# Which engine makes the low parts of the expert weights: VectorE alone, or VectorE with one in twelve on GpSimd

## The reference, cut to what matters

```
def moe_ffn(h, router, w1, w3, w2):              # h: 256 tokens x 1024
    logits = (t @ router).astype(float32)
    top_v, top_i = lax.top_k(logits, TOP_K)      # 2 of 8
    top_w = softmax(top_v)
    gates = sum(one_hot(top_i, 8) * top_w[..., None], axis=1)
    for e in range(N_EXPERTS):
        out = out + gates[:, e:e + 1] * (silu(t @ w1[e]) * (t @ w3[e])) @ w2[e]
```

## Time and profile before

| what | value |
|---|---|
| median of 3 runs | 1508.79 us (1505.52 to 1510.47) |
| the profiled execution: its time, its span | 1508.79 us, 1507.1 us |
| PE busy over the span | 1450.7 us (96%) |
| DVE | 1264.5 us (84%) |
| ACT | 1099.1 us (73%) |
| POOL | 91.9 us (6%) |
| DMA, mean over the span | 310 GB/s |
| DMA, in the expert stage from 700 to 1400 us | 416 GB/s |

### The profile page before, as it was taken

How to read it: one execution, slowest core, us unless ns; L and a number is a source line. 1 busy time by engine, 2 the same in 40 slices (tenths; PEclk the granted TensorE clock), 3 DMA queues, 4 the chain that set the end, 5 groups by cost and what they waited for, 6 DMA issues and landing times.

```text
span 1507.1 us, 22229 instructions
## 1 busy us (share of the span) xinstructions
PE 1450.7 (96%) x8401; PEld 1258.1 (83%) x8401; DVE 1264.5 (84%) x1414; ACT 1099.1 (73%) x1315; POOL 91.9 (6%) x48
## 2 busy tenths in 40 slices
PE   7999989999999999899999999999999999999996
PEld 7999969999899998788877877787877887778774
DVE  5887775455578868789999999999999999999996
ACT  5685553333547663588888888888898889898885
POOL 4000000000000000000000031000040000040001
PEclk9999999999999999999999999999999999999999
DMA  9545345555344443989999999999999999999993
GB/s 276 204 148 188 141 154 210 193 177 189 140 169 176 176 156 138 389 325 422 411 421 408 409 420 416 421 420 408 411 413 423 421 409 407 422 415 421 421 420 106
DMA packets 66439, 467.02 MB, mean 310 GB/s; under 512 B 7658, under 2 KB 7894, under 8 KB 11030
## 3 DMA queue, kind: packets, MB, share of 16 engines
q1 hardware_dynamic: 63878, 458.27, 76.0%
q0 software_dynamic: 2400, 7.24, 2.4%
q10 hardware_dynamic: 48, 0.02, 0.0%
HBM read 460.26 MB, written 5.24 MB: 309 GB/s over the span
## 4 chain that ended last, share of the span: by engine, by line
PE 71%; DVE 19%; ACT 6%; issue 2%; DMA 1%; POOL 0%; ACTq 0%; DVEq 0%
DVE w_lo L653 12%; PE bank L843 9%; PE bank L1150 9%; PE bank L844 9%; PE bank L845 9%; PE bank L1151 9%; PE bank L1154 9%; PE bank L1106 4%; PE bank L1103 4%; PE bank L1115 1%; ACT w_hi L581 1%; PE bank L1219 1%; ACT w_hi L647 1%; DVE w_lo L589 1%; PE bank L896 1%
## 5 line engine op out<-in xcount | busy, mean ns | idle before, releaser
L653 DVE TENSOR_TENSOR w_lo<-arena,w_hi 128x1024 fp32r<-128x1024 f32 x528 | 617.7, 1218 | 28.9 <-ACT w_hi L647 23.9
L647 ACT ACTIVATE w_hi<-arena 128x1024 fp32r<-128x1024 f32 x528 | 533.6, 1054 | 59.4 <-PE bank L1154 56.1
L589 DVE TENSOR_TENSOR w_lo<-ring,w_hi 128x2048 fp32r<-128x2048 f32 x94 | 214.9, 2290 | 129.7 <-ACT w_hi L581 128.7
L843 PE MATMUL bank<-h_hi,w_hi 128*128 128x256 f32 x992 | 283.2, 285 | 1.9 <-DVE h_lo L1729 1.7
L844 PE MATMUL bank<-h_lo,w_hi 128*128 128x256 f32 x992 | 280.6, 283 | 0.0
L845 PE MATMUL bank<-h_hi,w_lo 128*128 128x256 f32 x992 | 280.6, 283 | 0.0
L581 ACT ACTIVATE w_hi<-ring 128x2048 fp32r<-128x2048 f32 x94 | 179.7, 1913 | 105.4 <-PE bank L845 80.0
L843 PEld LDWEIGHTS bank<-h_hi,w_hi 128*128 128x128 f32 x992 | 190.2, 192 | 4.1 <-issue 2.9
L844 PEld LDWEIGHTS bank<-h_lo,w_hi 128*128 128x128 f32 x992 | 190.3, 192 | 0.5
L845 PEld LDWEIGHTS bank<-h_hi,w_lo 128*128 128x128 f32 x992 | 190.2, 192 | 0.0
L1150 PE MATMUL bank<-w_hi,h_hi 128*128 128x512 f32 x448 | 177.3, 396 | 1.6 <-DVE h_lo L2170 1.6
(11 more groups left out here) (313 smaller groups left out, 2193.7 us busy)
## 6 DMA issues: line engine op xcount, KB each, us to landing
arena<-in_moe_w SPq DMA_DIRECT2D x270, 1024.0 KB, 11.3
ring<-in_moe_w SPq DMA_DIRECT2D x66, 1024.0 KB, 11.4
ring<-in_ffn_w SPq DMA_DIRECT2D x33, 1024.0 KB, 4.8
ring<-in_w_gate SPq DMA_DIRECT2D x32, 1024.0 KB, 4.8
ring<-in_w_in SPq DMA_DIRECT2D x15, 1024.0 KB, 6.1
ring<-in_w_branch SPq DMA_DIRECT2D x8, 1024.0 KB, 4.8
ring<-in_w_out SPq DMA_DIRECT2D x8, 1024.0 KB, 4.8
x_tok<-in_x SPq DMA_DIRECT2D x2, 512.0 KB, 3.8
```

Source lines behind the costliest of these rows:

```text
L589: nc.vector.tensor_tensor(w_lo[:, m % LO, :], raw, w_hi[:, m % HI, :].bitcast(F32), ALU.subtract)\
L647: nc.scalar.activation(half_hi[:, r % AHEAD, :], raw_of(n)[:, HALF * (m % 2):HALF * (m % 2) + HALF], ACT.Copy)\
L653: eng.tensor_tensor(half_lo[:, r % AHEAD, :], raw_of(m // 2)[:, HALF * (m % 2):HALF * (m % 2) + HALF], half_hi[:, r % AHEAD, :].bitcast(F3 ...
L843: pe.matmul(out_, a[0], b[0], start=start, stop=False)
```

## The change

1. `half_whole`, `h_few` and `ex.rank` go. Every half is split, 672 on ACT. In a few step PE has two L1103 and two L1106 for the half that had two L1115.
2. GpSimd makes one low part in each of the first 53 steps: the third half of w2, the eleventh of the step's twelve (`ex.pool`). It has a semaphore of its own, `pool_lo_done`, on which PE waits for these halves, and SP for the slots of their pieces. DVE makes the other 619. POOL's loop now walks through the halves; the gathers of rows and the additions to the result stand in it at fixed places.
3. The branch for all tokens keeps its sum in SBUF, and ACT stores it; POOL's additions then add zeros. It does not run here.

The core of the diff, without the second branch and the lines that only lose the argument `rank` or `r`:

```
-        self.whole = {self.first[("h1", i, 0)] + WHOLE_Q for i in range(STEPS) if is_few(i) and SEQ[i][1] in WHOLE_STEPS}
-        self.split = [m for m in range(self.halves) if m not in self.whole]
-        self.rank = {m: r for r, m in enumerate(self.split)}
+        self.pool = [self.first[("w2", i, 1)] for i in range(POOL_STEPS)]        # POOL_STEPS = STEPS - 3
+        self.vector = [m for m in range(self.halves) if m not in self.pool]
...
         def wait_half_lo(eng, m):
-            eng.wait_ge(half_lo_done, m + 1)
+            if m in ex.pool:
+                eng.wait_ge(pool_lo_done, ex.pool.index(m) + 1)
+            else:
+                eng.wait_ge(half_lo_done, ex.vector.index(m) + 1)
...
+        def split_half_lo(eng, m):
+            eng.wait_ge(half_hi_done, m + 1)
+            eng.tensor_tensor(half_lo[:, m % AHEAD, :], raw_of(m // 2)[:, HALF * (m % 2):HALF * (m % 2) + HALF],
+                              half_hi[:, m % AHEAD, :].bitcast(F32), ALU.subtract)\
+                .then_inc(pool_lo_done if m in ex.pool else half_lo_done, 1)
...
                     for m in (2 * (n - RAW), 2 * (n - RAW) + 1):
-                        if m in ex.whole:
-                            sp.wait_ge(half_used, m + 1)
-                        else:
-                            wait_half_lo(sp, m)
+                        wait_half_lo(sp, m)
...
+            for u in range(ex.halves):                                            # on POOL
+                kind, i, j = ex.loads[u // 2]
+                done = (kind, j, u % 2)
+                now_at = i + (kind == "w2")
+                if done == ("h3", 1, 1) and i >= 2 and SEQ[i - 2][1] == S_MOE - 1:
+                    add_rows(SEQ[i - 2][0])
+                if done == ("w2", 1, 1) and now_at < STEPS and SEQ[now_at][1] == 4 and SEQ[now_at][0] + 2 < E:
+                    fetch_rows(SEQ[now_at][0] + 2)
+                if u + AHEAD in ex.pool:
+                    split_half_lo(pool, u + AHEAD)
+            add_rows(E - 1)
...
                     m = ex.first[(kind, i, 0)] + q
-                    if m in ex.whole:
-                        half_whole(m, [(h_few[:, k, :], slice(MU * k, MU * k + MU), bank[b][:, :]) for k in range(2)])
-                        continue
...
             def next_lo(u):                                                       # on DVE
-                if u in ex.rank and ex.rank[u] + AHEAD < len(ex.split):
-                    r = ex.rank[u] + AHEAD
-                    split_half_lo(dve, ex.split[r], r, ex.split[r] - ex.split[r - 1])
+                if u + AHEAD < ex.halves and u + AHEAD not in ex.pool:
+                    split_half_lo(dve, u + AHEAD)
```

More of the change, by code:

```diff
@@ L801, in _, with add_rows @@
             pool.wait_ge(xn_stored, 16 * TT)
[L802 to L805, removed]
+            def add_rows(e):
                 if e in SMALL:
@@ L1106, in half_few @@
                     last = pe.matmul(dst, both, wl[:, cols], start=False, stop=final(x))
[L1107 to L1115, removed]
                 last.then_inc(half_used, 1)
@@ L1143, in outer_few, with half @@
                     half_few(ex.first[("w2", i, 0)] + c, outs, lambda x: first and c == 0, lambda x: final and c == 3)
-            def half(m, r, outs, first, final):
-                pe.wait_ge(half_hi_done, r + 1)
-                w, wl = half_hi[:, r % AHEAD, :], half_lo[:, r % AHEAD, :]
+            def half(m, outs, first, final):
+                pe.wait_ge(half_hi_done, m + 1)
+                w, wl = half_hi[:, m % AHEAD, :], half_lo[:, m % AHEAD, :]
                 for x, (hi, lo, cols, dst) in enumerate(outs):
@@ L1155, in half, with inner @@
                 last.then_inc(half_used, 1)
-            def inner(kind, i, tiles, rank, gathers=None):
+            def inner(kind, i, tiles, gathers=None):
                 for q in range(4):
@@ L1164, in inner, with outer @@
                     m = ex.first[(kind, i, 0)] + q
-                    half(m, rank(m), outs, lambda x: q == 0 and x % 2 == 0, lambda x: q == 3 and x % 2 == 1)
-            def outer(i, acts, rank, first, final, amid=None):
+                    half(m, outs, lambda x: q == 0 and x % 2 == 0, lambda x: q == 3 and x % 2 == 1)
+            def outer(i, acts, first, final, amid=None):
                 for c in range(4):
@@ L1173, in outer @@
                     m = ex.first[("w2", i, 0)] + c
-                    half(m, rank(m), outs, lambda x: first and c == 0, lambda x: final and c == 3)
+                    half(m, outs, lambda x: first and c == 0, lambda x: final and c == 3)
             def gather(e, c, b):
@@ L1265, in gathered_experts @@
                         else:
-                            inner("h3", i, [(tile, 6)], ex.rank.get)
+                            inner("h3", i, [(tile, 6)])
                         if coming is not None:
@@ L1307, in all_tokens @@
                     if i < STEPS:
-                        inner("h1", i, [(tiles[t], 4 + t) for t in range(TT)], int)
-                        inner("h3", i, [(tiles[t], 6 + t) for t in range(TT)], int)
+                        inner("h1", i, [(tiles[t], 4 + t) for t in range(TT)])
+                        inner("h3", i, [(tiles[t], 6 + t) for t in range(TT)])
                     if i >= 1:
@@ L1574, in gathered_hi @@
                 n = FEW if e in SMALL else CAP
-                if e in SMALL and c == 1:
-                    act_e.wait_ge(h_few_zero, 1)
-                    fn(h_few[:, :, 0:FEW], bank[b][:, :].rearrange("p (k n) -> p k n", k=4)[:, FEW_K:FEW_K + 2, 0:FEW], ACT.Copy)
                 fn(h_hi[:, 4 * c:4 * c + 4, CAP * (e % 2):CAP * (e % 2) + n],
@@ L1661, in all_tokens @@
                         last.then_inc(acth_done, 1)
-                    next_hi_all(u)
+                    next_hi(u)
+                act_e.wait_ge(x_added, 4 * STEPS)
+                act_e.wait_ge(scattered, 16 * E)
+                for t in range(TT):
+                    act_e.dma_start(out[0, P * t:P * t + P, :], x_tok[:, t, :]).then_inc(whole_stored, 16)
+                act_e.wait_ge(whole_stored, 16 * TT)
             act_e.wait_ge(most_ready, 1)
@@ L2153, in next_lo @@
             def next_lo(u):
-                if u in ex.rank and ex.rank[u] + AHEAD < len(ex.split):
-                    r = ex.rank[u] + AHEAD
-                    split_half_lo(dve, ex.split[r], r, ex.split[r] - ex.split[r - 1])
-            def next_lo_all(u):
-                if u + AHEAD < ex.halves:
-                    split_half_lo(dve, u + AHEAD, u + AHEAD)
+                if u + AHEAD < ex.halves and u + AHEAD not in ex.pool:
+                    split_half_lo(dve, u + AHEAD)
             def gathered_lo(e, c, b):
```

75 lines of the change are left out of this document (26 added, 49 removed).

## The result

The changed kernel takes 1543.91 us (median of four runs, 1537.42 to 1545.93), the kernel before 1508.1 us: ratio 1.0228, 95% interval 1.0208 to 1.0249. It is slower by about 35 us (35.8 by these medians, 37.1 between the two profiled executions); the forecast was 1532, slower by 23.

What follows compares the result with a forecast made beforehand. PE, DVE and the DMA engines stood within 4%, DVE last in few-token steps. DVE's 81 us of hold less 42 us of parts, less 16 us absorbed by idle time, gave 23 us: 1508.8 + 23 = 1532 us, range 1498 to 1565.

Steps and rivals of the forecast that it cites:

- The hold: Expert stage: POOL's subtractions block DVE's low parts; 81 of POOL's 106 us hold DVE up, chance 0.5.
- The forecast's doubt: A POOL gather took 1.67 us beside four DVE low parts, so some POOL accesses might not wait.
- POOL's duration: Each of POOL's 53 subtractions of 128x1024 takes 2.0 us, with ends of 1.1 and 2.2 us.
- The sum on DVE: Expert stage: 81 us of hold less 42 us of parts taken away, 39 us more on DVE.
- The idle time that takes up delay: Half of DVE's 32 us idle over the stage, 16 us, absorbs delay, leaving 23 us.
- Few steps grow by about 0.8 us, many hardly: Sign of the forecast: nearly all of the 23 us falls in steps with few tokens.
- The reading of the earlier trace: 1108.58 to 1123.14 was taken as a step with few tokens, with DVE busy for all 14.56 us.
- PE's 13 us: Splitting 16 whole halves saves PE 0.82 us each, in few steps where DVE is last; counted as nothing.
- Faster: Rival: POOL runs beside DVE, the stage goes as fast as the loads; about 1501 us, chance 0.25.
- Starved: Rival: POOL gets in only when DVE is idle, not beside `lower`; about 1590 us, chance 0.11.
- The time to landing: Sign of the forecast: weight loads' time from issue to landing falls in the stage instead of growing.
- POOL's queue: Low parts behind POOL's indirect DMAs may come late three times, 0 to 9 us; counted as nothing.

Runs made afterwards that it cites:

- e12: Changed kernel, still 53 low parts on GpSimd, those in steps of many tokens moved from the eleventh to the seventh half: 1553.08 us.
- e3: Changed kernel, but GpSimd copies the raw weights into its 53 low parts instead of subtracting, one operand read: 1510.03 us.
- e2: Changed kernel, but GpSimd fills its 53 low parts with zeros, reading nothing: 1510.44 us.
- e5: Changed kernel with GpSimd's low part only in steps of many tokens (26 parts), VectorE making the others: 1544.78 us.
- e6: Changed kernel with GpSimd's low part only in steps of few tokens (27 parts), VectorE making the others: 1513.93 us.
- e1: Changed kernel with no low part on GpSimd; VectorE makes all 672 and no half stays whole: 1518.55 us.
- e4: Kernel before, with the whole half in all 28 steps of few tokens instead of 16: 1503.23 us.
- e9: Changed kernel with ten zero-weight products on PE before its wait for the activations' low part: 1536.99 us.
- e11: Changed kernel with GpSimd's part only in steps of many tokens, at the seventh half instead of the eleventh: 1534.29 us.
- e10: Changed kernel with zeros for GpSimd's 53 low parts and nobody making those halves' high parts: 1510.34 us.

## Why the prediction was right, and where it was not

- **The hold: right.** POOL's and DVE's subtractions exclude each other, as the three additions in the earlier trace rows had suggested. The Trainium skill ("SBUF — State Buffer", "Who interferes with whom") has this rule, and the trace agrees: a DVE part is stretched from 1.21 to up to 3.38 us, POOL's from 2.40 to 5.02, and in e12 to 12.01. The forecast's doubt, the gather that ran free in the earlier trace rows, said nothing about a subtraction.
- **POOL's duration: too small.** 2.40 us free of DVE, not 2.0 and outside the ends of 1.1 and 2.2. The rows were of 128 and 512 columns with one input. Their 1.08 us for one input was close (e3's copy takes 1.05); the second operand costs more than the first. In the Trainium skill, "GPSIMD Engine Reference", section 3.1, gives 4497 ns for 2048 columns, and its half, an estimate of 2.25 us, was nearer.
- **The sum on DVE: too large.** 81 us of hold were forecast, 63.7 are measured as stretched parts. Less the 42 us of parts not made that is 22 us, where the forecast had 39. That 22 is close to the forecast's 23 (39 - 16) is chance.
- **The idle time that takes up delay: wrong, the step that failed.** 16 us of DVE's idle time were to absorb the hold. It grew instead, from 0.56 to 1.53 us in a slow turn; only in a fast turn did it fall, from 0.56 to 0.20. e2 shows the growth with no hold at all (2.38). DVE idles where it is six halves ahead, and what it does not make there isn't stored for the fast turn. "Few steps grow by about 0.8 us, many hardly" came out in PE's turns: 1.02 in the fast ones, and of the 0.58 in the slow ones most is the clock. What was wrong is which parts cause it: e5 and e6, with parts in one kind of step only, came out the other way round than expected.
- **The reading of the earlier trace rows under it: wrong.** The stretch 1108.58 to 1123.14 was called a few step and DVE's. PE's records from 1104.2 to 1121.6 are of the long pieces, and that row has PE busy for all of its 14.56 us as well. Cut from product to product on DVE, a window mixes PE's two turns; cut at PE's own lines it shows a slow turn in which PE never stands and a fast one in which it does.
- **PE's 13 us and the sixteen halves, "nothing": wrong.** e1 puts splitting them at 11 us (some 6 of it the clock in its trace), and e4 gives 4.3 us for twelve more whole ones. In a fast turn PE waits for DVE and ACT; a whole half gives it 0.82 us of work in place of waiting and takes a part from both.
- **The clock: missing.** The forecast has no term for it. In the stage before there was no fall in the profiled execution; after has seven, and they cost 11 of the 37 us between the two profiled executions, the turns say. Since e1 has four, the falls are not GpSimd's work alone: they come with PE's longer waits. All runs agree, not only the profiled ones: the mean granted clock is 0.991 to 0.998 before, 0.989 to 0.992 in e1, 0.985 to 0.987 after and 0.990 to 0.997 in e9.
- **The rivals.** *Faster* would not have come out even without a hold: with DVE 42 us lighter and GpSimd's operation only 0.95 us long, e2 stands at 1510, not 1501; the loads, the bound named there, were not reached (415 GB/s, as before). *Starved* did not happen in the changed kernel: PE's weight loads wait for a low part 2.4 us in 700, and none of POOL's parts takes over 5.02 us. But it is real: with other places, in e12, three parts took up to 12.01 us and PE stood. The time to landing fell from 11.3 to 7.8 us, as said.
- **POOL's queue: right.** No addition was stuck, the one of the earlier trace rows took 2.17 us.
- **The number.** That 1544 lies in the range is in part luck: the hold was put 17 us too high, while 16 us were taken off for DVE's idle time, and the whole halves and the clock were put at nothing.

By runs: +11 us for splitting all halves (e1), +33 for what reading does and for the longer operation (after less e2), -8 for DVE's relief (e1 to e2). The clock is inside these: the traces have no fall before, four in e1, one in e2 and seven after, at about 1.5 us each.

**Still open.** How much of a hold's price each place in the turn has: e5, e6 and e11 have an order that fits, but e11's amount does not follow. Why GpSimd gets in at `lower` elsewhere and not in three cases of e12. What keeps e2 and e10 at 1510 with both DVE and ACT relieved: PE's waits there are for `lower` (14.9 us in e2), whose chain runs from the hidden product over PE's transposition and ACT's high part to DVE; no run shortened that chain, so it is argued, not shown. What decides whether a wait is followed by a fall of the clock.

The best version is e4, the kernel before with a whole half in all seven steps of each expert with few tokens instead of four of them: 1503.2 us.

## What to carry to other kernels

When two engines run coupled by a buffer of fixed depth and the consumer's pace alternates, cut the trace at the consumer's own fast and slow turns: relief or delay of the producer counts by where in the turn it falls, and the mean busy share says little. Before a part of VectorE's work is given to GpSimd, compare the duration of GpSimd's operation with the hole it leaves in VectorE's stream: a copy as long as the hole was free here (1.05 us), 53 subtractions of over twice that cost more than the work they took over, though the 27 of e6 did not. When TensorE is the consumer and begins to stand, its clock may fall too (here 1.5 us a time), so look at the granted clock before a wait is counted only by its length.

## What the runs showed of the hardware

- The exclusion of the subtractions goes both ways. GpSimd's one-operand copy waits as well: 1.05 us alone and about 2.05 beside a DVE part. A fill, which reads nothing, took 949 to 957 ns in all 53 cases.
- GpSimd's subtraction of 128x1024 with both inputs in SBUF: 2.40 us, twice DVE's 1.21.
- A subtraction on GpSimd can be kept waiting past DVE's instructions with an operand in PSUM: 10.84, 12.01 and 12.00 us in e12, until DVE stood. In the changed kernel the longest was 5.02, with `lower` beside it.
- An addition of rows by indirect DMA on GpSimd took 17.85 us before, in a stretch where DVE never paused, and 2.17 us in the changed kernel, where the holes are more frequent.
- Each of the seven stretches of 3.41 us at 1.2 GHz in the stage began at the end of a wait of PE for the low activations, or within 1.5 us of it; these waits were 2.03 to 3.47 us long. One of 2.04 us (ending at 1186.3) had no fall behind it. Before, the same wait was at most 1.4 us; three others of 2.2 us (for L2170) had no fall either, while in e1 the same three waits of 2.2 us had one each. So the length of the wait alone does not decide. By the turns that it falls in, a fall costs 1.3 to 1.7 us. With ten products of zero weights, 0.11 us each, before the wait, one was left.
